# Inverses of the 8x8 diagonal blocks on VectorE, in compact columns with shuffles, in place of two rounds and one level on TensorE

## What is computed

```python
def step(S, inp):                      # S (B,H,64,64), per token
    r_t, w_t, k_t, v_t, a_t, b_t = inp
    sa = jnp.einsum('bhij,bhj->bhi', S, a_t)
    S = S * w_t[..., None, :] + sa[..., :, None] * b_t[..., None, :] + v_t[..., :, None] * k_t[..., None, :]
    o = jnp.einsum('bhij,bhj->bhi', S, r_t)
    return S, o
...
S, o = _wkv7_scan(wkv0, rh, decay, kh, vh, -kk, kk * ah)
on = ((o - mu) * lax.rsqrt(var + GN_EPS)).reshape(B, T, R) * lw['ln_w'] + lw['ln_b']
y_a = (on + bonus.reshape(B, T, R)).astype(x.dtype) * jax.nn.silu(g_rwkv)
```

## Time and profile before

| | |
|---|---|
| time, median of 3 runs | 1307.97 us (1307.15 to 1308.64) |
| the profiled execution | 1319.9 us, of which the span of its instructions is 1318.3 us |
| TensorE busy | 1257.5 us (95% of the span) |
| VectorE busy | 728.2 us (55%) |
| ScalarE busy | 547.1 us (41%) |
| TensorE's granted clock, mean | 0.974 of full speed |

### The profile page before, as it was taken

One profiled execution on the slowest core, in us unless ns is written; L12 is line 12 of the kernel. 1 busy time (PEld: TensorE's weight loads), 2 busy tenths in 40 slices (PEclk: granted clock), 3 DMA queues, 4 the chain that ended last, 5 costly groups with the idle time before them and its releaser, 6 DMA issues.

```text
span 1318.3 us, 22597 instructions
## 1 busy us (share of the span) xinstructions
PE 1257.5 (95%) x8460; PEld 1199.1 (91%) x8460; DVE 728.2 (55%) x1031; ACT 547.1 (41%) x871; POOL 243.9 (19%) x318
## 2 busy tenths in 40 slices
PE   2899999999999999999998899999999999979996
PEld 2789999999999999999998799999999799959995
DVE  3847575756757575665758554444444244485431
ACT  4335362626446372735435233333333333344331
POOL 3513140402113040402117200000000200051121
PEclk8899999999999999999999899999999799989998
DMA  9322333333332333243245355555555745516550
GB/s 265 95 81 68 110 80 93 94 101 89 90 104 75 112 83 95 73 120 91 65 121 153 103 145 155 148 144 142 159 144 156 205 128 144 149 34 177 154 145 27
DMA packets 274054, 155.44 MB, mean 118 GB/s; under 512 B 6933, under 2 KB 269629, under 8 KB 273364
## 3 DMA queue, kind: packets, MB, share of 16 engines
q1 hardware_dynamic: 267044, 137.50, 37.3%
q0 software_dynamic: 6976, 17.48, 5.1%
HBM read 149.57 MB, written 5.61 MB: 118 GB/s over the span
## 4 chain that ended last, share of the span: by engine, by line
PE 88%; DVE 6%; DMA 3%; SPq 1%; ACT 1%; issue 1%; POOL 0%; DVEq 0%; POOLq 0%; ACTq 0%
PE acc L1406 17%; PE acc L1407 17%; PE acc L1408 16%; PE wide L1408 5%; PE wide L1407 5%; PE wide L1406 5%; PE wide L1425 4%; PE wide L1565 3%; PE wide L1558 2%; PE wide L1483 1%; PE wide L1571 1%; DMA wraw<-in_w_in 1%; PE wide L1525 1%; DVE o L1366 1%; DMA pt<-in_p_sample 1%; DVE win_a L1248 1%
## 5 line engine op out<-in xcount | busy, mean ns | idle before, releaser
L978 DVE TENSOR_TENSOR wl<-wraw,wh 128x1024 fp32r<-128x1024 f32 x252 | 309.0, 1231 | 230.2 <-ACT wh L672 228.4
L672 ACT CAST wh<-wraw 128x1024 fp32r<-128x1024 f32 x256 | 267.8, 1047 | 299.6 <-PE acc L1408 208.7
L1406 PE MATMUL acc<-hh,wh 128*128 128x320 f32 (+1 forms) x1088 | 367.2, 338 | 6.0 <-DVE wl L978 4.0
L1407 PE MATMUL acc<-hl,wh 128*128 128x320 f32 (+1 forms) x1088 | 338.9, 311 | 0.0
L1408 PE MATMUL acc<-hh,wl 128*128 128x320 f32 (+1 forms) x1088 | 338.4, 311 | 0.0
L1406 PEld LDWEIGHTS acc<-hh,wh 128*128 128x128 f32 x1088 | 206.5, 190 | 10.2 <-issue 4.2
L1407 PEld LDWEIGHTS acc<-hl,wh 128*128 128x128 f32 x1088 | 206.5, 190 | 3.6
L1408 PEld LDWEIGHTS acc<-hh,wl 128*128 128x128 f32 x1088 | 205.6, 189 | 0.0
L1406 PE MATMUL acc<-x1h,wh 128*128 128x320 f32 x256 | 84.2, 329 | 5.8 <-DVE x1l L1362 5.8
L1407 PE MATMUL acc<-x1l,wh 128*128 128x320 f32 x256 | 80.8, 316 | 0.0
L1408 PE MATMUL acc<-x1h,wl 128*128 128x320 f32 x256 | 80.7, 315 | 0.0
(11 more groups left out here) (349 smaller groups left out, 2371.7 us busy)
## 6 DMA issues: line engine op xcount, KB each, us to landing
wraw<-in_w_in SPq DMA_DIRECT2D x160, 512.0 KB, 3.8
wraw<-in_w_branch SPq DMA_DIRECT2D x32, 512.0 KB, 3.9
wraw<-in_w_out SPq DMA_DIRECT2D x32, 512.0 KB, 3.9
wraw<-in_w_ple_gate SPq DMA_DIRECT2D x32, 512.0 KB, 3.9
xt<-in_x_prompt SPq DMA_DIRECT2D x2, 1024.0 KB, 5.2
S0n<-in_state_wkv POOLq DMA_DIRECT2D x16, 128.0 KB, 5.7
out<-so POOLq DMA_DIRECT2D x16, 128.0 KB, 2.8
xt<-in_x_prompt POOLq DMA_DIRECT2D x2, 1024.0 KB, 8.5
```

Source lines behind the costliest of these rows:

```text
L672: A.copy(wh[:, slot, :], wraw[:, slot, :]).then_inc(s["hi_ready"], 1)
L978: V.tensor_tensor(wl[:, slot, :], wraw[:, slot, :], wh[:, slot, :].bitcast(F32), ALU.subtract).then_inc(s["lo_ready"], 1)
L1406: M.matmul(out[:, 0:width], wh[:, slot, wcol], hi, start=first, stop=False)
L1407: M.matmul(out[:, 0:width], wh[:, slot, wcol], lo, start=False, stop=False)
```

## The change

The rounds and the first level are removed. VectorE computes the inverse of every 8x8 diagonal block by itself, in arrays that hold for each of the 64 rows only the 8 (or 4) columns of its own block. `Tm` is masked to 8x8 blocks (`inner`) and folded to 8 columns by a reduction. The inverses of its two 4x4 blocks are the sum of five terms (`terms`: the block, the identity, and products of one column with one row of it), where the rows are brought to all partitions of a block by `stream_shuffle`. The off-diagonal 4x4 block is the product of inverse, block and inverse, made in two steps, each of four shuffles, a multiplication and a reduction. The last instruction spreads the 8 columns over 64 (`Y`). Three levels remain, all with four groups. The order of work changes with it: `go(3)` is called ahead of the score masks on both engines, `out(1)` follows the new code on VectorE, `ARK` comes ahead of `ABD`, which now signals `ark_ready`, and TensorE issues the 11 units of the removed steps in one piece (`inner`).

The new arrays lie where `rn` and `cl` are, free at that time; only `terms` is new space. The constants gain 14 columns (row masks, unit vectors) and the mask tables lose 512 columns.

```diff
-ROUNDS = 2
-LEVELS = 4
-SMALL = 1
+LEVELS = 3
+OCT = 8
...
+    put(CM, m, "inner", (s // OCT == t // OCT) & (s < t) & seq)
...
+                go(3)
...
-                go(3)
+                out(1)
...
+            def quad_row(k):
+                return [4 * (i // 4) + k for i in range(32)]
+
+            def oct_row(k):
+                return [OCT * (i // OCT) + k for i in range(32)]
...
                 out(0)
+                go(3)
...
-                V.tensor_tensor(Tm[:, :, :], sb[:, :, 0, :], cms("quads").rearrange("p (g c) -> p g c", g=G), ALU.mult
-                                ).then_inc(s["dve_step"], 1)
-                dve.wait_ge(s["dve_step"], r * 6 + 1)
-                V.tensor_tensor(Y[:, :, :], Tm[:, :, :], istk.unsqueeze(1).to_broadcast([P, G, C]), ALU.add).then_inc(s["y_ready"], 1)
+                V.tensor_tensor(Tm[:, :, :], sb[:, :, 0, :], cms("inner").rearrange("p (g c) -> p g c", g=G), ALU.mult
+                                ).then_inc(s["base_step"], 1)
+
+                def stepped(n):
+                    dve.wait_ge(s["base_step"], r * BASE_STEPS + (n + 1))
+
+                stepped(1)
+                V.tensor_reduce(inner[:, :, :], Tm[:, :, :].rearrange("p g (o e) -> p g e o", e=OCT), mybir.AxisListType.X, ALU.add
+                                ).then_inc(s["base_step"], 1)
                 V.tensor_tensor(ARB[:, :, :], sb[:, :, 1, :], cms("incl").rearrange("p (g c) -> p g c", g=G), ALU.mult)
+                stepped(2)
+                diag = terms[:, :, 0, :]
+                V.scalar_tensor_tensor(diag, inner[:, :, 4:8], cfs("lowers"), inner[:, :, 0:4], ALU.mult, ALU.add
+                                       ).then_inc(s["base_step"], 1)
+                stepped(3)
+                V.tensor_scalar(cross[:, :, :], inner[:, :, 4:8], cfs("upper"), None, ALU.mult).then_inc(s["base_step"], 1)
+                for k in range(2):
+                    V.stream_shuffle(rows2[:, :, k, :], diag, quad_row(k + 1)).then_inc(s["base_step"], 1)
+                stepped(6)
+                V.tensor_tensor(terms[:, :, 2:4, :], terms[:, :, 0, 1:3].unsqueeze(3).to_broadcast([P, G, 2, 4]),
+                                rows2[:, :, :, :], ALU.mult).then_inc(s["base_step"], 1)
                 dve.wait_ge(s["score_ps"], r * 3 + 2)
                 V.tensor_tensor(AKBD[:, :, :, :], sk[:, :, 0, :].unsqueeze(2).to_broadcast(bd),
                                 cms("strict").rearrange("p (g h c) -> p g h c", g=G, h=2), ALU.mult)
+                stepped(7)
+                V.tensor_tensor(terms[:, :, 4, :], terms[:, :, 2, 2:3].to_broadcast([P, G, 4]), rows2[:, :, 1, :], ALU.mult
+                                ).then_inc(s["base_step"], 1)
+                V.tensor_tensor(ARK[:, :, :], sk[:, :, 1, :], cms("incl").rearrange("p (g c) -> p g c", g=G), ALU.mult)
+                stepped(8)
+                V.tensor_reduce(quad[:, :, :], terms[:, :, :, :].rearrange("p g k j -> p g j k"), mybir.AxisListType.X, ALU.add
+                                ).then_inc(s["base_step"], 1)
                 dve.wait_ge(s["score_ps"], r * 3 + 3)
                 V.tensor_tensor(ABD[:, :, :, :], B[4][:, 0:T].rearrange("p (g c) -> p g c", g=G).unsqueeze(2).to_broadcast(bd),
-                                cms("lower").rearrange("p (g h c) -> p g h c", g=G, h=2), ALU.mult)
-                V.tensor_tensor(ARK[:, :, :], sk[:, :, 1, :], cms("incl").rearrange("p (g c) -> p g c", g=G), ALU.mult
+                                cms("lower").rearrange("p (g h c) -> p g h c", g=G, h=2), ALU.mult
                                 ).then_inc(s["ark_ready"], 1)
...
-                for i in range(ROUNDS):
-                    dve.wait_ge(s["t_ps"], r * (LEVELS + ROUNDS) + i + 1)
-                    V.tensor_tensor(Tm[:, :, :].rearrange("p g c -> p (g c)"), B[0][:, 0:T], cms("quads"), ALU.mult
-                                    ).then_inc(s["dve_step"], 1)
-                    dve.wait_ge(s["dve_step"], r * 6 + (i + 2))
-                    V.tensor_tensor(Y[:, :, :], Tm[:, :, :], istk.unsqueeze(1).to_broadcast([P, G, C]), ALU.add
-                                    ).then_inc(s["y_ready"], 1)
-                    if i == 0:
-                        go(3)
+                stepped(9)
+                V.tensor_scalar(octo[:, :, 0:4], quad[:, :, :], cfs("upper"), None, ALU.mult).then_inc(s["base_step"], 1)
+                for k in range(4):
+                    V.stream_shuffle(rows4[:, :, k, :], quad[:, :, :], oct_row(4 + k)).then_inc(s["base_step"], 1)
+                V.tensor_scalar(parts[:, :, 4, :], quad[:, :, :], cfs("lowers"), None, ALU.mult).then_inc(s["base_step"], 1)
+                stepped(14)
+                V.tensor_tensor(parts[:, :, 0:4, :], cross[:, :, :].unsqueeze(3).to_broadcast([P, G, 4, 4]), rows4[:, :, :, :],
+                                ALU.mult).then_inc(s["base_step"], 1)
+                stepped(16)
+                V.tensor_reduce(half_way[:, :, :], parts[:, :, 0:4, :].rearrange("p g k j -> p g j k"), mybir.AxisListType.X,
+                                ALU.add).then_inc(s["base_step"], 1)
+                stepped(17)
+                dve.sem_inc(s["waits"], 1)
+                for k in range(4):
+                    V.stream_shuffle(rows4b[:, :, k, :], half_way[:, :, :], oct_row(k)).then_inc(s["base_step"], 1)
+                stepped(21)
+                V.tensor_tensor(parts[:, :, 0:4, :], octo[:, :, 0:4].unsqueeze(3).to_broadcast([P, G, 4, 4]), rows4b[:, :, :, :],
+                                ALU.mult).then_inc(s["base_step"], 1)
+                stepped(22)
+                V.tensor_reduce(octo[:, :, 4:8], parts[:, :, :, :].rearrange("p g k j -> p g j k"), mybir.AxisListType.X,
+                                ALU.add).then_inc(s["base_step"], 1)
+                stepped(23)
+                V.tensor_tensor(Y[:, :, :].rearrange("p g (o e) -> p g o e", e=OCT),
+                                octo[:, :, :].unsqueeze(2).to_broadcast([P, G, C // OCT, OCT]),
+                                cfs("octs").unsqueeze(1).unsqueeze(3).to_broadcast([P, G, C // OCT, OCT]), ALU.mult
+                                ).then_inc(s["y_ready"], 1)
+                out(1)
...
                 def turned(n):
-                    gs = G if n < SMALL else GP
-                    dve.wait_ge(s["y_ready"], r * (LEVELS + ROUNDS + 1) + (ROUNDS + n + 1))
+                    dve.wait_ge(s["y_ready"], r * (LEVELS + 1) + n + 1)
                     for h in range(2):
-                        V.transpose(XBD[half(h), 0:gs, h, :], Y[half(h), 0:gs, :]).then_inc(s["x_ready"], 1)
+                        V.transpose(XBD[half(h), 0:GP, h, :], Y[half(h), 0:GP, :]).then_inc(s["x_ready"], 1)
 
                 for n in range(LEVELS):
-                    w = T if n < SMALL else TP
                     turned(n)
-                    if n:
-                        go(3 + n)
-                    dve.wait_ge(s["t_ps"], r * (LEVELS + ROUNDS) + (ROUNDS + n + 1))
-                    V.tensor_tensor(Tm[:, :, :].rearrange("p g c -> p (g c)")[:, 0:w], B[0][:, 0:w],
-                                    cm[:, lv + n * T:lv + n * T + w], ALU.mult).then_inc(s["t_ready"], 1)
-                    if n == 0:
-                        out(1)
-                    if n == 3:
+                    go(4 + n)
+                    dve.wait_ge(s["t_ps"], r * LEVELS + n + 1)
+                    V.tensor_tensor(Tm[:, 0:GP, :].rearrange("p g c -> p (g c)"), B[0][:, 0:TP],
+                                    cm[:, lv + n * TP:lv + (n + 1) * TP], ALU.mult).then_inc(s["t_ready"], 1)
+                    if n == 2:
                         out(2)
                     dve.wait_ge(s["m_ps"], r * LEVELS + n + 1)
-                    Yf = Y[:, :, :].rearrange("p g c -> p (g c)")[:, 0:w]
-                    V.tensor_tensor(Yf, B[1][:, 0:w], Yf, ALU.add).then_inc(s["y_ready"], 1)
-                go(3 + LEVELS)
+                    Yf = Y[:, 0:GP, :].rearrange("p g c -> p (g c)")
+                    V.tensor_tensor(Yf, B[1][:, 0:TP], Yf, ALU.add).then_inc(s["y_ready"], 1)
+                go(4 + LEVELS)
...
-                for i in range(ROUNDS):
-                    pe.wait_ge(s["y_ready"], r * (LEVELS + ROUNDS + 1) + i + 1)
-                    for g in range(G):
-                        last = M.matmul(B[0][:, tok(g)], flat(ABD, g), Y[:, g, :], start=True, stop=True)
-                    last.then_inc(s["t_ps"], 1)
-                    st.advance(AFTER["series"])
+                st.advance(AFTER["inner"])
```

More of the change, by code:

```diff
@@ L104 @@
 N_CF = _columns(CF, ("ident", P), ("istk", HD), ("ones2", P), ("mean2", P), ("meand", P), ("segment", T),
-                ("batch", NB), ("eps", 2), ("count", 4 * 16))
-N_CM = _columns(CM, ("quads", T), ("incl", T), ("strict", 2 * T), ("lower", 2 * T), ("level", LEVELS * T))
+                ("batch", NB), ("eps", 2), ("count", 4 * 16), ("upper", 1), ("lowers", 1), ("unit", 4), ("octs", OCT))
```

(45 more changed lines are left out.)

13 lines of the change are left out of this document (7 added, 6 removed).

## The result

| | before | after |
|---|---|---|
| time, median | 1307.93 us (4 runs, 1307.15 to 1308.64) | 1296.95 us (4 runs, 1294.90 to 1298.81) |
| ratio after / before | | 0.9895, 95% interval 0.9862 to 0.9927 |
| the profiled execution | 1319.9 us, span 1318.3 | 1294.9 us, span 1292.9 |
| mean granted clock | 0.974 | 0.979 |

The kernel is faster by 11.0 us. The two profiled executions lie 25 us apart, which is more than the change: that of before has a wait near the end of the program which has nothing to do with it (experiment 5), and that of after is the fastest of its four.

A forecast was written before the change was run, and what follows sets the result against it. TensorE was taken to bound the mixer, with `ark_ready` the tight wait. 35.0 us saved less 19.0 stall and 6.8 clock gave 9.2 us less, forecast 1299; own case 1293 to 1305 (chance 0.56), whole range 1286 to 1312.

The forecast's parts named there:

- What bounds it: In the mixer TensorE bounds, and VectorE work added ahead of `ark_ready` stalls it at once.
- Rival D: At `ABD` in the mixer: VectorE arrives in time, no wait, all 35 us are saved: 1273; chance 0.05.
- The saving on TensorE: From first round to first four-group product, 9.42 us become 5.04: 4.38 us saved a pair, 35.0 in eight.
- The stall's sum: VectorE work added ahead of `ark_ready` sums to 2.38 us; TensorE stalls 2.4 a pair, 19 in all.
- What comes behind: VectorE after `ABD`: eight shuffles hidden by 2.5 us; first product and tile 3's first unit wait for nothing.
- The clock: Behind the mixer's stalls: four of eight bring the clock down, each costing 1.7 us, 6.8 us in all.
- Rival B: In the mixer the clock holds despite the stalls, so 16 us are saved: 1292; chance 0.22.
- rival C: Between `Tm` and `ABD` small operations don't overlap: stall 3.1 us, clock falls in every pair, slower, 1311; chance 0.17.
- The whole sum: Over eight pairs: 35.0 saved, less 19.0 in stalls and 6.8 in clock, 9.2 us less.

The follow-up runs named there:

- experiment 5: Kernel after with the four score masks right behind `Tm`, `go(3)` and the inverse behind `ark_ready`, and the x loads on their own semaphore (late wait split): 1268.46 us.
- experiment 1: Kernel after with the four score masks directly behind `Tm`, and `go(3)` and the whole inverse behind `ark_ready`: 1278.78 us.
- Experiment 9: experiment 5 with the 8x8 inverse left out, `Y` being `Tm` plus the identity in one operation: 1268.86 us.
- experiment 6: Kernel after with only TensorE's late wait split, the x loads having a semaphore apart from those of p: 1296.37 us.
- experiment 2: Kernel after with only `go(3)`, the remainder of chunk 6, moved behind `ABD` on VectorE: 1281.65 us.
- experiment 4: Kernel after with one more VectorE operation ahead of `ABD`, a second 640-element mask into an array nothing reads: 1315.68 us, ratio 0.9997 to the kernel before.
- experiment 7: Kernel before with only TensorE's late wait split, the x loads having a semaphore apart from those of p: 1307.99 us.
- experiment 10: experiment 5 with one more VectorE multiplication of 640 elements, 0.74 us, between `ABD` and `go(3)`, into an array nothing reads: 1273.84 us.

## Why the prediction was right, and where its terms were off

1299 was predicted and 1296.95 measured, in the range and on the right side. The steps:

**What bounds it** held: TensorE in the mixer, with VectorE's `ark_ready` as the tight wait. The stall stands where it was put, behind `ABD`, 19.2 us in all where 19.0 was predicted. Rival D (no wait) is out.

**The saving on TensorE** was 4.38 us a pair and is 4.9 (experiment 1: 75.04 - 70.13) to 5.07 (72.48 - 2.51 against 75.04). The stretch for which the term was made is nearly exact: from the place of the first round (336.78 + 0.55) to the product are 4.95 us, where I had 5.04. The missing 0.3 to 0.5 and more lies behind that product. I had taken the levels that remain as equal, and they run a little faster: from the first product to the tail 364.49 - 351.75 = 12.74 before, by the starts of the groups, and 12.43 after. This is the term that was mis-sized most, 4 us or more over eight pairs. Nearly all of the 0.31 lies at the first of these updates. Timeline of TensorE, before:

```profile
353.82 0.31 PE L1408 MATMUL acc<-hh,wl 128*128 128x320 f32 x1
354.15 1.10 PE L1565 MATMUL wide<-Tm,vBD 128*128 128x64 f32 x8
```

and after:

```profile
344.34 0.31 PE L1468 MATMUL acc<-hh,wl 128*128 128x320 f32 x1
344.49 1.00 PE L1625 MATMUL wide<-Tm,vBD 128*128 128x64 f32 x8
```

The old update starts 0.33 behind the matmul ahead of it and is 1.10 long, the new one 0.15 and 1.00, together 0.28. In the old kernel the remainder of a chunk (352.46, 1.22 long) kept VectorE's mask for this update until 353.60 + 0.42 = 354.02; in the new one that mask starts at 343.31 and ends well ahead. The old kernel had small waits of this kind, and with the rounds gone this one is gone too. Two more, some 0.36 together, stand near the end of the old pair (from the products with `sq` at 403.40 on). In this pair the kernel after and experiment 5 don't have them and experiment 1 does, which makes the difference between its 70.13 and the 69.73 of experiment 5.

**The stall's sum** came out right, 2.38 against 2.42, by errors that cancel. The remainder 1.13 (1.14 predicted), the products and masks within 0.03. Two shuffles with what they wait for take 332.38 - 332.08 = 0.30, where I had 0.64: one starts 0.09 behind the other though its pattern is new, and the loading of the pattern is a row of 0.01. The lower bound, 0.21 each, was not low enough. The estimate by the Trainium skill's figure ("VectorE: DVE Perf Modes", section "The perf-mode tier table"), some 0.3 a shuffle, is three times the 0.09 from one to the next and nearly twice the 0.17 that one lasts. On the other side the fold of `Tm` costs 0.68 to the next operation, where a multiplication of as many elements lets it go after 0.40, so 0.27 more than I had; the reduction of 100 elements 0.23 and not 0.17; `cross` and the diagonal blocks 0.10 more together. That the two sides meet is luck.

**What comes behind** held: no wait for `Y`, for tile 3's first unit or for a shuffle is in the kernel after. Experiment 9 shows it outright for the masks-first order.

**The clock.** Four falls at 1.7 us were predicted; the profile has three, and that of experiment 6 five, at 1.6. Rival B (no fall) and the eight falls of rival C are both out for these executions. The prediction's reason, a stall near the shortest that brings the clock down, is borne out by the series of stalls in the mixer: 1.2 to 1.4 us none of eight (experiment 2), 2.1 to 2.5 three or five of eight, 2.8 to 3.3 all eight (experiment 4). Within the middle group the length doesn't decide: the falls come behind every second stall from the second or third on, in the kernel after and in experiment 6. So "half of them" was the right size, and the prediction had no reason for it but that the length was near a limit. For other surroundings the limit doesn't hold: in experiment 1 a wait of 1.73 us ahead of transposes was enough.

**Rival C's premise**, that small operations don't overlap, is refuted by the earlier trace rows as before and by the rows after: from `cross` (0.23 long, at 331.92) to the first shuffle 0.16, `ARB` to the next after 0.39 for 0.48, shuffle to shuffle 0.09 for 0.17. Only what waits for a result starts behind its end (`cross` 0.27 behind the start of `terms`, 0.23 long). The prediction gave the rule of the Trainium skill ("VectorE: DVE Perf Modes", section "The DRAIN you can't avoid") by its first half: the same section adds that a next operation which isn't held starts earlier. With this addition the trace agrees.

**The whole sum** with measured terms: 8 x 4.9 = 39.2 saved, 19.2 lost in stalls, 3 x 1.6 = 4.8 in the clock, leaves 15.2; with the five falls and 18.4 of experiment 6 it is 12.8. The medians give 11.0 and 11.6. Most of what is missing can be found by the starts of TensorE's steps in the kernel after and in experiment 7, the kernel before without the late wait. The spans are 13.3 us apart (1292.9 and 1306.2). The transposes of `bBD` in the first pair come 2.1 us later (115.79 and 113.70), which is the first stall. From there to the eighth pair's the kernel after takes 512.49 us and not 524.53, 12.0 less: seven savings of 4.9 less seven stalls of 2.4 and three falls of 1.6 give 12.7. The eighth pair saves 4.7 (from its `bBD` to the transposes of `uS` that follow the mixer, 48.5 and 53.2). Then 1.2 us are lost between those transposes and the late ones of x (343.7 and 342.5), where the program is the same; that this stretch isn't equally long from kernel to kernel is seen in the profiles, and why is not shown. The other 2 us are no part of the sum: the profiled execution of the kernel after is the fastest of its four, 2.05 below their median. Whether the slower ones had more falls isn't known, since one execution of it was profiled.

So the number owes something to luck. The saving was taken 4 us too small and the clock's loss 2 us too large. By the sum alone that would have made the kernel 6 us faster than predicted, and it is 2 us faster.

## What to carry to other kernels

A change that takes work from the engine that bounds the kernel and gives it to another must be placed as well as sized: here the same operations give 11.6 us in one order and 39.5 in another (experiments 6 and 5, both against experiment 7), because the first puts 2.4 us of them ahead of a signal on which the bounding engine waits at once. Look first for the tightest wait on the helper engine, send its signal first, and put everything that isn't wanted yet behind it. Then price a stall of TensorE with what the clock takes after it, since that can cost two thirds of the stall again. And take the price of a short wait from start to start: the idle time in the row leaves out the overlap that is lost (0.36 in the row, 0.62 in the time, experiment 10).

## What was unexpected of the hardware

- A `STREAM_SHUFFLE` of 20 elements takes 0.17 us with the next 0.09 behind it, and a `LOAD_MASK_SELECT` ahead of it 0.01: shuffles with changing patterns are as cheap as any small operation.
- A `TENSOR_REDUCE` that reads 320 elements by a stride takes 0.76 us where a multiplication of 320 takes 0.48; one that reads 100 takes 0.32.
- Stalls of equal length brought the clock down behind some and not behind others, for the most part in turn: in the kernel after four of 2.51 to 2.53 us in a row, with falls behind two of them, and in experiment 6 seven of 2.33 us, with falls behind four.
- A wait of 1.73 us ahead of 48 transposes left the clock at 1.2 GHz through nearly all of them, 13.76 us in place of 9.15 (experiments 1 and 5), while stalls of 2.5 us in the mixer, with dense matmuls behind, cost 1.6 when the clock fell. What runs behind a wait seems to decide its price more than its length does; no run here changes the one without the other.
